# Down weights of two expert stages loaded as one transfer each, instead of two halves

## The reference, cut to what matters

```
for g in range(N_GROUPS):                                   # 4 groups of 8 experts: 32 experts
    h = (jax.nn.silu(jnp.einsum('td,edf->tef', t, w_gate[g]))      # d = 1024, f = 512
         * jnp.einsum('td,edf->tef', t, w_up[g]))
    out = out + jnp.einsum('tef,efd->td', h * combine[:, g, :, None], w_down[g])
```

## Time and profile before

| | |
|---|---|
| median of 3 runs | 1740.8 us (1740.01 to 1745.42) |
| the profiled execution | 1749.01 us |
| its span, first to last instruction | 1747.0 us |
| PE busy | 1610.4 us (92%) |
| DVE, ACT busy | 519.7 us (30%), 261.7 us (15%) |
| chain that ended last | PE 57%, DMA 32% (31% `in_e_up`), DVE 7% |
| read from memory | 568.22 MB, 326 GB/s over the span |
| mean granted TensorE clock | 0.966 of full speed |

### The profile page before, as it was taken

One profiled execution on the slowest core, in us unless ns is written; L12 is line 12 of the kernel. 1 busy time (PEld: TensorE's weight loads), 2 busy tenths in 40 slices (PEclk: granted clock), 3 DMA queues, 4 the chain that ended last, 5 costly groups with the idle time before them and its releaser, 6 DMA issues.

```text
span 1747.0 us, 30552 instructions
## 1 busy us (share of the span) xinstructions
PE 1610.4 (92%) x12492; PEld 809.7 (46%) x12493; DVE 519.7 (30%) x1187; ACT 261.7 (15%) x516; POOL 28.3 (2%) x73
## 2 busy tenths in 40 slices
PE   7998998877788999999999999898999999999996
PEld 5486754543466453434333333674444343333332
DVE  6986343100028352111111111323451121111122
ACT  2303111000014320011010110223211010111010
POOL 4000000100000000000000000000000000000000
PEclk9998999988898999999999999899999999999999
DMA  6323459999982069999999999722489999999995
GB/s 243 132 110 145 178 211 400 420 421 421 421 350 108 25 259 416 422 421 422 421 422 422 422 422 423 312 98 95 157 318 422 422 422 421 422 422 422 422 422 222
DMA packets 79204, 570.25 MB, mean 326 GB/s; under 512 B 8848, under 2 KB 12320, under 8 KB 14368
## 3 DMA queue, kind: packets, MB, share of 16 engines
q1 hardware_dynamic: 75168, 561.14, 78.3%
q10 hardware_dynamic: 3968, 8.17, 1.4%
HBM read 568.22 MB, written 1.05 MB: 326 GB/s over the span
## 4 chain that ended last, share of the span: by engine, by line
PE 57%; DMA 32%; DVE 7%; issue 2%; SPq 1%; ACT 1%; ACTq 0%; DVEq 0%; PEldq 0%
DMA space<-in_e_up 31%; PE psum L997 19%; PE psum L1036 7%; PE psum L758 7%; PE psum L766 5%; PE psum L1049 4%; PE psum L914 3%; PE psum L821 2%; PE psum L1339 2%; PE psum L1295 2%; DVE space L2320 1%; PE psum L810 1%; PE psum L782 1%; PE psum L799 1%; PE psum L1259 1%
## 5 line engine op out<-in xcount | busy, mean ns | idle before, releaser
L997 PE MATMUL psum<-space 128*32 128x512 f32 (+2 forms) x5120 | 524.2, 564 | 63.0 <-DMA space<-in_e_up 52.8
L997 PEld LDWEIGHTS psum<-space 128*32 128x32 f32 x5120 | 169.5, 113 | 412.8 <-issue 400.3
L1036 PE MATMUL psum<-space 128*32 128x512 f32 (+1 forms) x2304 | 257.1, 597 | 5.2 <-DMA space<-in_e_down 5.1
L1982 DVE TENSOR_TENSOR space<-space,psum 128x512 f32<-128x512 f32 (+1 forms) x40 | 25.4, 634 | 585.6 <-PE psum L997 585.6
L758 PE MATMUL psum<-xT,space 128*128 128x256 f32 x704 | 159.7, 390 | 7.2 <-DMA space<-in_stream 3.0
L758 PEld LDWEIGHTS psum<-xT,space 128*128 128x128 f32 x704 | 137.2, 196 | 28.3 <-issue 8.8
L1049 PE MATMUL psum<-space 128*128 128x512 f32 x320 | 148.0, 605 | 0.0
L1036 PEld LDWEIGHTS psum<-space 128*32 128x32 f32 x2304 | 71.9, 110 | 161.1 <-issue 161.1
L1049 PEld LDWEIGHTS psum<-space 128*128 128x128 f32 x320 | 57.5, 189 | 90.9 <-issue 90.9
L1989 DVE COPY space<-psum 128x512 f32<-128x512 f32 x40 | 27.7, 692 | 230.4 <-PE psum L1036 230.4
L914 PE MATMUL psum<-space,xT 128*128 128x128 bf16 x1024 | 89.4, 219 | 0.0
(11 more groups left out here) (358 smaller groups left out, 1298.4 us busy)
## 6 DMA issues: line engine op xcount, KB each, us to landing
space<-in_e_gate SPq DMA_DIRECT2D x160, 1024.0 KB, 20.5
space<-in_e_up SPq DMA_DIRECT2D x160, 1024.0 KB, 20.7
space<-in_e_down SPq DMA_DIRECT2D x160, 1024.0 KB, 20.6
space<-in_stream SPq DMA_DIRECT2D x26, 2048.0 KB, 14.5
rows<-in_rows ACTq DMA_DIRECT2D x9, 512.0 KB, 8.3
x_sb<-in_x SPq DMA_DIRECT2D x2, 512.0 KB, 4.1
space<-in_mem ACTq DMA_DIRECT2D x1, 1024.0 KB, 17.4
xT<-in_stream ACTq DMA_DIRECT2D x1, 1024.0 KB, 7.6
```

The costliest lines, as they stand in the source:

```text
L997: last = mm(psum[r, 5 + g, 0:FW], xg[:, u, k, r], w, start=(k == 0), stop=(k == KD - 1))
L1036: last = mm(psum[r, (4, 7)[half], :], hT[:, f, r], w, start=(f == 0), stop=(f == F - 1))
```

## The change

In stages 2 and 3 the down weights (weights 4 and 5) are loaded whole, each with one transfer of 2 MB and one signal, on the `loaded` semaphore of the slot's first half. SP waits, for each of them, until PE has used the second half, and then issues the whole. PE waits for both whole weights ahead of the first down matmul, and no more in between. PE still gives back both halves, each with its own `used`. The order of the weights on SP stays as it was; gate and up stay in two halves. The counts of loads (`loads`) leave out the two half slots that no longer get a signal (9 and 11). Stage 1, whose weights were whole already, is as before.

```diff
--- before.py
+++ after.py
@@ -435,6 +435,9 @@
         for s in range(2 * NSLOT + 2):
             if part:
                 n = 8 if s // 2 in (0, EXTRA_SLOT // 2) else 16
+                if s in (9, 11):
+                    moe_uses[s] += n
+                    continue
             else:
                 n = 8 * (s < EXTRA_SLOT)
             loads[s] += n
@@ -572,13 +575,17 @@
                         sp.wait_ge(used[hs], i * per + (base[hs] + at_u + SEED))
                         load_expert(w, hs, step)
                     return
-                for part_ in range(3):
+                for part_ in range(2):
                     for half in range(2):
                         for w in (2 * part_, 2 * part_ + 1):
                             if w:
                                 hs, per, at_u = slots[w]
                                 sp.wait_ge(used[hs + half], i * per + (base[hs + half] + at_u + SEED))
                                 load_half(w, hs + half, step, half)
+                for w in (4, 5):
+                    hs, per, at_u = slots[w]
+                    sp.wait_ge(used[hs + 1], i * per + (base[hs + 1] + at_u + SEED))
+                    load_expert(w, hs, step)
                 if more:
                     hs = moe_slots(e, 1 - u)[0][0]
                     for half in range(2):
@@ -601,7 +608,7 @@
                 hs = moe_slots(e, 0)[w][0]
                 if moe_after[e][hs // 2]:
                     full(sp, *last_use[moe_after[e][hs // 2]])
-                if e == "e1":
+                if e == "e1" or w >= 4:
                     load_expert(w, hs, 0)
                 else:
                     for half in range(2):
@@ -1021,9 +1028,6 @@
                                  [((0, 1), 0), ((0, 1), 1), ((2, 3), 0), ((2, 3), 1)]):
                     if 0 in fs:
                         moe_wait(pe, e, ("xgA", "xgB")[half], c(2))
-                    elif half == 0:
-                        for x in range(X):
-                            arrived(2 * X + x, 1)
                     for f in fs:
                         for n in blocks:
                             r = slice(n * BLOCK, (n + 1) * BLOCK)
```

## The result

The changed kernel took 1751.18 us (median of 8 runs, 1745.64 to 1754.75) against 1744.17 us for the kernel before in the same comparison (8 runs): ratio 1.0038, 95% interval 1.0023 to 1.0054. By the ratio that is 6.6 us slower (4.0 to 9.4 by its interval), where 9.4 were forecast.

A forecast was written before the change was run, and what follows sets the result against it. It took DMA transfer at 421 to 423 GB/s to bound stages 2 and 3. Terms of +6.8, +5.7 and -3.1 us gave +9.4 us, from 1740.8 to 1750.2 us (+0.54%); 8-in-10 range 1743.0 to 1758 us.

The forecast's parts named there:

- What bounds the stage: Stages 2 and 3: transfer sets 29.85 us a step; only idle DMA, PE work after the last load or rate cost time.
- Part 1: First step of stages 2 and 3: down issued 3.4 us later leaves the DMA idle that long, +6.8 us in all.
- In the middle of a stage no: Mid-stage, down issued 3.4 us later finds the queue still full, over 15 us of loads ahead, so no cost.
- Part 2: Last step of stages 2 and 3: PE's wait for both whole down weights costs +2.9 and +2.8 us, +5.7 in all.
- Part 3: Down transfers of 15 reloading steps in two stages: 16 KB rows at 426 GB/s save 0.10 us a step, -3.1 us.
- Part 4: Fewer PE waits and SP issues per step, down's first loads as one DMA, stage 1 untouched: no effect on time.
- the rival by which two transfers fewer would save 4 us a step: Every step: at 2.0 us per DMA plus bytes over 436 GB/s, two DMAs fewer save some 120 us in all.
- one cost hidden: The first-step hole or the end wait costs nothing: +2.6 or +3.7 us; chance 0.18, together with no effect.
- The queue that runs dry in every step: The 3.4 us paid 15 times in each stage, +102 us, 1840 us; chance 0.06, including dry once more per stage.
- The faster side: Down transfers of steps 1 to 15 run over 440 GB/s, winning back 12.5 us; 1735.6 us at 448; chance 0.04.

The follow-up runs named there:

- pe_waits_both: Kernel before, with PE waiting for both halves of both down weights ahead of the first down matmul, SP untouched: ratio 1.0042, stretches of stages 2 and 3 together +6.3 us.
- late_release: Kernel before, with SP issuing down's first halves only once the second halves are used too, PE's waits unchanged: ratio 1.0034, both stretches together +6.1 us.
- last_in_halves: Changed kernel, with down in halves in each stage's last step and PE's last pair of steps written out: ratio 1.0046 to the kernel before, stretches +4.3 us.
- rows_8k: Changed kernel, with each 2 MB down transfer carrying 256 rows of 8 KB instead of 128 of 16 KB: ratio 1.0058 to the kernel before, stretches +11.8 us.
- gate_ahead_once: Changed kernel, with SP issuing the next gate weight ahead of down in each stage's first step only: ratio 1.0028 to the kernel before, stretches +2.7 us.

## Why the prediction came out as it did

- **What bounds the stage**: right. The chain, ten waits of 1.6 us, a step that changed only with the transfer rate, and pe_waits_both (15.5 us of waits, 3 us of cost) all show it. One thing is missing in the rule that time is lost only by idle DMA, by work behind the last load or by rate: a stall of PE two steps ahead of the end also costs, since PE can't win it back in time.
- **Part 1, the hole in the first step, +6.8**: right. late_release alone gives +6.1, with 3 us of idle DMA visible. "In the middle of a stage no" held as well: the windows there are full.
- **Part 2, the wait at the end, +5.7**: right in place and size, alone +6.3. The forecast put all of it on the last step; last_in_halves got back only 2.6 us there, and it took the last two steps to get back 4.6.
- **Part 3, -3.1**: right in sign and cause, the size was off: -5.0 (rows_8k against the changed kernel). The forecast took 426 GB/s from two windows of 23 and 24 us; down's 16 KB rows move at 429 by the step. It lay near the lower bound (-5.8). The Trainium skill's 3 cycles a packet (DMA: Bandwidth & Descriptors, "Bandwidth") come to 0.6%, an estimate; measured are 1.7%, and the measurement decides.
- **Part 4**: right as far as the runs can tell. rows_8k has two transfers and two signals fewer a step than late_release and the same step of 29.83 us. This also answers the rival by which two transfers fewer would save 4 us a step. The fit that it took from the Trainium skill (DMA: Bandwidth & Descriptors, "Anatomy of one DMA") is stated there for transfers issued by GpSimd; here SP issues them.
- **The rivals**: "one cost hidden" is excluded by two runs. The queue that runs dry in every step did not appear; in the second step it did, for some 2 us, only once the gate had been moved ahead (gate_ahead_once). The faster side needed over 440 GB/s; 429 came.
- **What was to be seen**: the place of the waits and the hole came (3 us near zero, about 4 forecast), and so did the start of stage 2's last down block (453.7 us after the stage's first matmul, 455.7 forecast). 71012 packets were forecast, 69988 came, since the 16 small packets of each transfer had been left out. 424 GB/s came where about 423 was forecast.

The effect was 6.6 us where 9.4 were forecast, and most of the difference is part 3, for which the forecast granted 1.9 us too little. The rest is within the scatter. That the time itself, 1751.18, is within 1 us of the forecast 1750.2 is luck: the kernel before took 1744.17 in the comparison, 3.4 us more than the median of three runs that the forecast started from, and this offset the 2.8 us by which the effect was overrated.

## What to carry to other kernels

In a stage bound by transfers, count three things: idle DMA time, PE work left behind the last landing, and the rate. Waits of the compute engine in the middle are free, and their total does not tell a cost (15.5 us of waits cost 3 us here). In this kernel coarser transfers cost time at the start, where all buffers are full and the queue is fed by release alone, and at the end; they gained only through longer rows. A lag of PE from one coarse wait is won back only at the difference of the two paces per step (1.7 us here), so a remedy in the last step alone may come too late.

## What was not expected of the hardware

Rows of 16 KB move at 429 GB/s where rows of 8 KB move at 421.6, both with the queue full and 2 MB in a transfer (rows_8k against the changed kernel). With all weights of a step in 16 KB rows the windows of stage 2 show 428:

```profile
904.00:994.00 90.00, 86.43 (x795) 33.55 (x788) 14.03 (x25) 9.40 (x14) 0.00 (x0) 1.00 1.01 428
```
